# The query and key heads of a two-layer decoder trunk turned by VectorE in 32x32 blocks, where TensorE turned them before

## The reference

```python
h = rms_norm(x, g);  z = h @ w_in          # u, v, c_q, c_kv, k_rope, two gates
A = gelu(z_u) * (w_s @ layer_norm(gelu(z_v)) + b)
q = (rms_norm(c_q) @ w_uq).reshape(B, S, 16, 96)
kv = (rms_norm(c_kv) @ w_ukv).reshape(B, S, 16, 128)
k = concatenate([kv[..., :64], broadcast(k_rope)]);  v = kv[..., 64:]
q = rope(rms_norm(q));  k = rope(rms_norm(k))
p = softmax(causal(q @ k.T / sqrt(96)));  B = p @ v
x = x + (sig(g_A) * (A @ P_A) + sig(g_B) * (B @ P_B)) @ w_out
x = x + channel_mixer(rms_norm(x))
```

## Time and profile before

| | |
|---|---|
| time, median of 3 runs | 1435.28 us (1435.23 to 1435.92) |
| the profiled execution | 1435.76 us, span 1434.0 us |
| PE busy | 1424.2 us (99%) |
| DVE busy | 1143.0 us (80%) |
| ACT busy | 961.3 us (67%) |
| bytes moved | 415 MB |
| attention stretch of layer 0, first scores to pa 1 0 | 120.75 to about 190 us |
| the same in layer 1 | 427.7 us later |

### The profile page before, as it was taken

The page is one execution under the profiler, slowest core; times in us unless marked ns, Lnnn a source line. Parts: engine busy times, 40 slices in busy tenths (PEclk is TensorE's granted clock), DMA queues, the critical chain, the costliest instruction groups (busy, mean ns, idle before and its releaser), DMA issues.

```text
span 1434.0 us, 19208 instructions
## 1 busy us (share of the span) xinstructions
PE 1424.2 (99%) x6747; PEld 1178.5 (82%) x6747; DVE 1143.0 (80%) x1160; ACT 961.3 (67%) x1003; POOL 45.2 (3%) x54
## 2 busy tenths in 40 slices
PE   9999999999999999999999999999999999999998
PEld 7888778888888888778888888888888888888886
DVE  6987756665546977756989899898898988989987
ACT  6676754544435676754677787777777777777775
POOL 2000003000000000000200000000000000000200
PEclk9999999999999999999999999999999999999999
DMA  9473348955465473447899999999999999999994
GB/s 338 158 239 118 118 153 302 337 179 172 164 209 193 147 236 117 132 162 262 297 386 415 387 359 410 384 380 409 360 398 372 385 414 382 381 380 412 372 396 164
DMA packets 163267, 415.13 MB, mean 290 GB/s; under 512 B 15420, under 2 KB 43960, under 8 KB 163176
## 3 DMA queue, kind: packets, MB, share of 16 engines
q1 hardware_dynamic: 157128, 393.42, 74.3%
q0 software_dynamic: 5008, 16.97, 3.6%
q10 hardware_dynamic: 1040, 3.68, 0.6%
HBM read 398.20 MB, written 15.81 MB: 289 GB/s over the span
## 4 chain that ended last, share of the span: by engine, by line
PE 95%; ACT 2%; DVE 2%; issue 0%; POOL 0%; DVEq 0%; ACTq 0%; POOLq 0%
PE ps L551 88%; PE ps L1095 1%; PE ps L825 1%; PE ps L968 1%; PE ps L947 1%; PE ps L955 1%; PE ps L869 1%; ACT w_hi L506 1%; ACT qk_t L1238 1%; PE ps L934 0%; PE ps L903 0%; PE ps L946 0%; ACT prob L1363 0%; ACT sq L1363 0%; ACT act_hi L1238 0%
## 5 line engine op out<-in xcount | busy, mean ns | idle before, releaser
L511 DVE TENSOR_TENSOR w_lo<-raw,w_hi 128x2048 fp32r<-128x2048 f32 (+3 forms) x240 | 500.9, 2105 | 138.7 <-ACT w_hi L506 136.3
L506 ACT ACTIVATE w_hi<-raw 128x2048 fp32r<-128x2048 f32 (+3 forms) x240 | 421.8, 1769 | 185.2 <-PE ps L551 170.9
L551 PE MATMUL ps<-w_hi,act_hi 128*128 128x512 f32 (+1 forms) x1264 | 333.3, 392 | 0.7 <-ACT act_hi L1238 0.6
L551 PE MATMUL ps<-w_hi,act_lo 128*128 128x512 f32 (+1 forms) x1264 | 331.2, 388 | 0.0
L551 PE MATMUL ps<-w_lo,act_hi 128*128 128x512 f32 (+1 forms) x1264 | 327.4, 387 | 0.0
L551 PEld LDWEIGHTS ps<-w_lo,act_hi 128*128 128x128 f32 x1264 | 235.6, 188 | 48.2
L551 PEld LDWEIGHTS ps<-w_hi,act_lo 128*128 128x128 f32 x1264 | 234.9, 188 | 47.5
L551 PEld LDWEIGHTS ps<-w_hi,act_hi 128*128 128x128 f32 x1264 | 232.3, 188 | 47.2 <-ACT act_hi L1238 1.4
L511 DVE TENSOR_TENSOR w_lo<-raw_more,w_hi 128x2048 fp32r<-128x2048 f32 (+1 forms) x96 | 201.8, 2110 | 30.1 <-ACT w_hi L506 30.0
L506 ACT ACTIVATE w_hi<-raw_more 128x2048 fp32r<-128x2048 f32 (+1 forms) x96 | 170.0, 1776 | 55.2 <-PE ps L551 54.3
L511 DVE TENSOR_TENSOR w_lo<-raw_low,w_hi 128x2048 fp32r<-128x2048 f32 (+1 forms) x64 | 137.6, 2156 | 11.5 <-ACT w_hi L506 11.0
(11 more groups left out here) (284 smaller groups left out, 1231.4 us busy)
## 6 DMA issues: line engine op xcount, KB each, us to landing
raw<-in_moe_w_gu SPq DMA_DIRECT2D x128, 512.0 KB, 9.0
raw_more<-in_moe_w_down SPq DMA_DIRECT2D x80, 512.0 KB, 7.0
raw<-in_w_in SPq DMA_DIRECT2D x72, 512.0 KB, 4.6
raw_low<-in_moe_w_gu SPq DMA_DIRECT2D x64, 512.0 KB, 10.3
raw_more<-in_moe_w_gu SPq DMA_DIRECT2D x64, 512.0 KB, 10.5
raw<-in_moe_w_gu SPq DMA_DIRECT2D x64, 384.0 KB, 7.3
raw<-in_moe_w_down SPq DMA_DIRECT2D x48, 512.0 KB, 6.7
raw<-in_dense_w_gu SPq DMA_DIRECT2D x44, 512.0 KB, 5.0
```

Of the source, the lines that this page charges most:

```text
L506: nc.scalar.activation(w_hi[:, self.split_slot(j), 0:n], self.raw(j)[:, 0:n], ACT.Copy).then_inc(self.hi, 1)
L511: nc.vector.tensor_tensor(w_lo[:, c, 0:n], self.raw(j)[:, 0:n], w_hi[:, c, 0:n].bitcast(F32), ALU.subtract).then_inc(self.lo, 1)
L551: return nc.tensor.matmul(dst, a, b, start=start and n == 0, stop=stop and n == 2)
```

## The change

`qb` and `kb` get the layout [partition, token tile, group of 32 columns, head, 32], so that a head's three groups of 32 columns lie apart. In place of `qk_turns`:

- When the queries are ready, POOL issues 12 DMAs that move 32-partition pieces of `qb` to `q_blocks` (in SBUF, 128 KB each); then 12 for the keys of the first eight heads to `k_lent`, and 12 for the others to `k_last` (64 KB each). They put group g of a block of 32 tokens on the partitions 32g to 32g+31.
- DVE transposes 32x32 blocks in place (`blocks`): `q_blocks` in two halves of eight heads, `k_lent`, `k_last`, each 96 x 2048.
- ACT copies the turned queries with the gain to `q_first` and `q_second` (four heads each), and the other eight (`last_q`) to `q_last`. PE reads keys straight from `k_lent` and `k_last`.
- `k_lent` lies on the fourth raw slot, so that the chunks from u 0 0 to ga 1 4 have three slots; the first chunk that takes the slot again waits for the scores of pair 3.
- `q_rope` stands behind uq 2 and ukv 0 (before: behind ga 0 0 and ga 0 4), the squares of the queries' second half directly behind uq 2's reading, the squares of the keys' first half before the reading of ukv 2; `k_scale` stands behind ukv 3 and, ahead of that step's split, behind ga 0 0 (before: behind u 0 0 and gb 1 4). The reading of a uq strip takes ACT three instructions, `k_scale` three on DVE.
- In the first expert the load of the next expert's rows moves three steps later and the slot weights get a tile of their own.

```diff
-        mul(l, "uq", 2, 0, [evac("uq", 2)])
+        mul(l, "uq", 2, 0, [evac("uq", 2), ("head_squares", l, "q", 1), ("q_rope", l, 0)])
+        mul(l, "ukv", 0, 0, [("q_rope", l, 1), evac("ukv", 0)])
         plan.append(("head_sums", l, "q", 1))
-        mul(l, "ukv", 0, 0, [evac("ukv", 0)])
         mul(l, "ukv", 1, 0, [evac("ukv", 1)])
-        plan.append(("head_sums", l, "k", 0))
-        mul(l, "ukv", 2, 0, [evac("ukv", 2)])
-        mul(l, "ukv", 3, 0, [evac("ukv", 3)])
-        plan.append(("head_sums", l, "k", 1))
-        mul(l, "ga", 0, 0, [("mix_tokens", l, 0)])
-        plan.append(("q_rope", l, 0))
+        mul(l, "ukv", 2, 0, [("head_sums", l, "k", 0), evac("ukv", 2)])
+        mul(l, "ukv", 3, 0, [evac("ukv", 3), ("head_sums", l, "k", 1), ("k_scale", l, 0)])
+        mul(l, "ga", 0, 0, [("mix_tokens", l, 0), ("k_scale", l, 1)])
         mul(l, "ga", 0, 4, [("mix_tokens", l, 1), evac("ga", 0)])
-        plan.append(("q_rope", l, 1))
-        mul(l, "u", 0)
-        plan.append(("k_scale", l, 0))
-        mul(l, "u", 0, 4, [("u_arg", l, 0), ("split", l, len(chunks)), ("u_gelu", l, 0)], split=False)
-        mul(l, "u", 1, 0, [("branch", l, 0), *slot(1, exps=False)], inside=[(4, turn(0))], split=False)
-        mul(l, "u", 1, 4, [("u_arg", l, 1), *slot(2)], split=False,
-            inside=[(2, ("a_turns", l, 0)), (2, ("softmax", l, 0)), (5, turn(1)), (5, split())])
+        plan.append(("blocks", l, "q", 0))
+        mul(l, "u", 0, 0, [("blocks", l, "q", 1)])
+        mul(l, "u", 0, 4, [("u_arg", l, 0), ("split", l, len(chunks)), ("u_gelu", l, 0), ("blocks", l, "k", 0)], split=False)
+        mul(l, "u", 1, 0, [("branch", l, 0), *slot(1, exps=False)], split=False)
+        mul(l, "u", 1, 4, [("u_arg", l, 1), ("last_q", l, "q", 1), ("blocks", l, "k", 1), *slot(2)], split=False,
+            inside=[(2, ("a_turns", l, 0)), (2, ("softmax", l, 0)), (5, split())])
...
+                def move_heads(to, src, heads, moved):
+                    for b in range(4):
+                        for g in range(DG):
+                            pool.dma_start(to[32 * g:32 * g + 32, b:TT * 4:4, :, :], src[32 * b:32 * b + 32, :, g, heads, :]
+                                           ).then_inc(moved, 16)
+
+                pool.wait_ge(q_ready, TT * (l + 1))
+                move_heads(q_blocks, qb, slice(0, H), q_moved)
+                pool.wait_ge(lo_done, lent_read[l] + 1)
+                pool.wait_ge(k_ready, 2 * l + 1)
+                move_heads(k_blocks[0], kb, slice(0, 8), k_moved[0])
+                pool.wait_ge(k_ready, 2 * l + 2)
+                pool.wait_ge(q_moved, 16 * 4 * DG * (l + 1))
+                move_heads(k_blocks[1], kb, slice(8, H), k_moved[1])
...
-                    wait_turn_read(pe, qk_turn[l, pair])
-                    wait_turn_read(pe, qk_turn[l, pair] + 1)
+                    if pair % 4 == 0:
+                        pe.wait_ge(q_scaled, 2 * l + pair // 4 + 1)
+                        pe.wait_ge(k_turned, 2 * l + pair // 4 + 1)
...
+                elif kind == "blocks":
+                    half = step[3]
+                    if step[2] == "q":
+                        dve.wait_ge(q_moved, 16 * 4 * DG * (l + 1))
+                        part, done = q_blocks[0:DQ, :, 8 * half:8 * half + 8, :].rearrange("p b h i -> p b (h i)"), q_turned
+                    else:
+                        dve.wait_ge(k_moved[half], 16 * 4 * DG * (l + 1))
+                        part, done = k_blocks[half][0:DQ].rearrange("p b h i -> p (b h i)"), k_turned
+                    nc.vector.transpose(part, part).then_inc(done, 1)
```

More of the change, by code:

```diff
@@ L74, in decoder_trunk @@
     HR = DR // 2
+    DG = DQ // 32
     E = moe_w_gu.shape[1]
@@ L482, in split_slot, with wait_slot @@
                 return (self.n0 + j) % SPLIT
-            def load(self, sp, e, j, pieces):
+            def wait_slot(self, sp, e, j):
                 r = len(self.slots)
@@ L704, in expert_loads @@
                 for d in range(len(EDOWN_K)):
-                    if not last and d == 2:
-                        if q == 0 and is_first(e):
-                            sp.wait_ge(pass_sems[0]["slot_read"], 1)
+                    if not last and d == (ROWS_AT if q or not is_first(e) else FIRST_ROWS_AT):
+                        if not q and is_first(e):
+                            sp.wait_ge(rows_written, 16 * 2 * TT)
                         rows_load(q, e + 1)
@@ L1325, in _ @@
                     turn_hi_parts(b0, hid_hi, 2 * step[2], 1.0)
-                elif kind == "head_sums":
+                elif kind == "head_squares" or kind == "head_sums" and step[2:] != ("q", 1):
                     hf = step[3]
@@ L1366, in _ @@
                     op.then_inc(exp_done, 1)
-                elif kind == "qk_turns":
-                    pair, b = step[2], b0
-                    if pair:
-                        act.wait_ge(scores_done, PAIRS * l + pair)
-                    for hh in range(2):
-                        act.wait_ge(turn_done, b + hh + 1)
-                        if not l and not pair and not hh:
-                            act.wait_ge(qk_gain_ready, 1)
-                        copy(qk_t[0:DQ, hh, 0:S], ps[0:DQ, 4 + (b + hh) % 2, 0:S], qk_gain[0:DQ, l:l + 1])
-                        copy(qk_t[0:DQ, hh, S:2 * S], ps[0:DQ, 4 + (b + hh) % 2, S:2 * S]).then_inc(turn_free[(b + hh) % 2], 1)
+                elif kind == "last_q" or kind == "blocks" and step[2:] != ("q", 1):
+                    if step[2] == "q":
+                        half = step[3]
+                        act.wait_ge(q_turned, 2 * l + half + 1)
+                        if not l and not half:
+                            act.wait_ge(qk_gain_ready, 1)
+                        if half:
+                            for i in range(2):
+                                act.wait_ge(k_moved[i], 16 * 4 * DG * (l + 1))
+                        scale = qk_gain[0:DQ, l:l + 1]
+                        turned_blocks = q_blocks[0:DQ, :, 8 * half:8 * half + 8, :].rearrange("p b h i -> p h b i")
+                        for to, a in ((q_last, 0),) if half else ((q_first, 0), (q_second, 4)):
+                            n = to.shape[1]
+                            op = copy(to[0:DQ].rearrange("p h (b i) -> p h b i", i=32), turned_blocks[:, a:a + n], scale)
+                        op.then_inc(q_scaled, 1)
                 elif kind in ("split", "split_hi"):
@@ L1504, in slot_weights @@
                 def slot_weights(e):
-                    if q or not is_first(e):
-                        act.wait_ge(z["xw_landed"], 16 * gathers(q, e))
-                    else:
+                    if not q and is_first(e):
                         act.wait_ge(z["first_weights"], 16)
+                        copy(slot_w[:], xw_first[:, 0:1]).then_inc(z["slot_read"], 1)
+                        return
+                    act.wait_ge(z["xw_landed"], 16 * gathers(q, e))
                     copy(slot_w[:], xw[:, e:e + 1] if isinstance(e, int) else xw[:, bass.ds(e, 1)]).then_inc(z["slot_read"], 1)
@@ L1525, in body @@
                         split(e, c + LEAD, last)
-                        if c == SLOT_READ:
+                        if c == SLOT_READ and (q or not first):
                             slot_weights(e)
@@ L1533, in body @@
                             turn_part(e, EGS - 1)
+                        if first and not q and d == FIRST_SLOT_READ:
+                            slot_weights(e)
                         if not last and d in (6, 8):
```

170 lines of the change are left out of this document (109 added, 61 removed).

## The result

| | before | after |
|---|---|---|
| median | 1435.6 us (4 runs, 1435.23 to 1436.32) | 1444.24 us (4 runs, 1444.16 to 1445.21) |
| profiled span | 1434.0 us | 1442.4 us |
| granted clock, mean | 1.0 | 0.995 |

The account below looks back on a forecast made before the run. PE, busy 1424.2 of 1434.0 us, was taken as the bound. Per layer 1.5 + 5.0 + 1.4 - 0.3 + 0.5 - 7.1 = +1.0, two layers +2.0, clock +2.0: 1439.3 us, range 1430.5 to 1443.0.

Parts of the forecast that it names:

- What goes: PE's sets of eight transposes: 0.89 us saved a set, eight sets a layer, 7.1 us each, 14.2 us in all.
- Step 1: PE's wait at ga 0 0, in the banks of ukv 2, which ACT reads behind the key squares: +1.5 us a layer.
- Step 2: PE's wait before the first scores, from the DVE, ACT, DVE chain ending in the k_lent transpose: +5.0 us a layer.
- Step 3: PE's wait for pair 1's probabilities, with DVE transposing k_last ahead of the maximum: +1.4 us, old 0.3 wait included.
- Step 4: Shared banks: PE's second transposition of the probabilities waits longer for DVE's bt_lo, +0.5 us; later slots costed at no wait.
- Hidden: Moves of queries and keys, three slots instead of four, and first expert's loads: thought hidden, nothing costed.
- The clock: PE restarting at half clock after the 5 us stop loses about 2 us, taken in one of two layers: +2.0.
- The rival of both layers: PE restarts at the lower clock after the long wait in both layers: 1441.3 us; chance 0.14.
- that the clock holds: Rival: PE's waits stay but its clock does not fall behind them: 1437.3 us; chance 0.25.
- Cheap transposes: Rival: DVE transposes cost under 1.8 us (or chain shorter), pause under 3 us, clock holds: 1430.7 us; chance 0.20.
- Moves late: Rival: queries' moves land after DVE wants them, up to 5 us more a layer: 1447 us; chance 0.08.

Follow-up runs that it names:

- e3: Changed kernel with ACT reading ukv 2 from PSUM before it squares the keys; 1443.85 us, ratio 1.0045 to the kernel before.
- e7: Changed kernel with POOL holding the queries' moves until the low part of the split of ga 0 4 is done; 1450.71 us, ratio 1.0095.
- e4: Changed kernel, hand-over reordered: ACT splits u 1 4 before copying queries, DVE turns k_lent earlier, low part of gb 1 0 later; 1432.6 us, ratio 0.997.
- e8: Changed kernel with only DVE's turn of k_lent moved ahead of the addition for u 0's argument; 1439.19 us, ratio 1.0016.
- e2: Changed kernel with DVE's transpose of k_last moved from ahead of pair 1's maximum to behind pair 3's; 1441.9 us, ratio 1.0033.
- e1: Changed kernel with 40 unused transposes on PE ahead of the first scores of each layer; 1439.86 us, ratio 1.0025.
- e6: e4 with e2's edit, and q's second and k's head sums and two splits' low parts placed later; 1428.08 us, ratio 0.9934.
- e9: e8 with the edit of e2 (last keys turned late); 1435.79 us, ratio 0.9993 to the kernel before.
- e5: e4 with the edits of e2 and e3; 1428.83 us, ratio 0.9939 to the kernel before.

## Why the prediction was right and where it failed

**What goes:** right. From 159.55 to 193.47 four sets less give back 3.5 us (7.65 - 4.19), 0.87 a set against 0.89.

**Step 1:** the place and the releaser were right, the size nearly. Forecast +1.5, measured a wait of 1.70 and a shift of 2.05 at ga 0 0. The second square of the keys starts at 89.27 where 88.85 was worked out. e3 confirms the cause: with the reading ahead of the squares, ACT's `vv` releases nothing any more. But e3 also shows that this step and step 2 don't simply add: of the 0.8 us won here, 0.4 and 0.7 were left at the first scores.

**Step 2:** the chain was right link by link, its sum 1.3 us short: first scores at 127.66, forecast 126.3. 0.96 of that is there at its start (109.96 for 109.0): 0.55 from ga 0 0, and 0.4 because ACT comes to the split of u 1 0 late, behind the chunk that landed late (e7, without that delay, starts at 109.63). Of the other 0.4, the copies are 0.2: their steps were 1.07 and 1.03 us and not 0.93 each. The transposes were priced right: 2.28 to 2.30 us in the records, with steps of 2.2, as taken. The wait itself is 5.57 and 5.16 us against 5.0. e4 and e8 show that this chain was the largest single cost, and that it came from the order of two queues, not from the turns: e4 does all the same turns.

**Step 3:** right, 1.30 and 1.27 for 1.4; e2 removes it. **Step 4:** 0.44 in place of 0.17, so +0.3 a layer where 0.5 was taken, and from pa 0 0 on there is no wait, as costed.

**Hidden:** failed in part, though small. The queries' moves were in time (DVE turns at 112.17 right behind a split), but I asked only when they land and not what they do to others. The loads beside them land in 7.8 us (median) instead of 4.6, and one weighs on step 2, as e7 shows. The Trainium skill (SBUF — State Buffer, the section SBUF: two separate sides) warned of another thing, POOL kept from its descriptors by VectorE's copies in a two-port mode. The trace shows no sign of it, with the queries' 12 issues at 0.54 us each while DVE is busy 6.07 of 6.45 us; but DVE's work there is `tensor_tensor`, sums and a few operations on 32 columns, and no such copy, so it is hardly a test of the warning. The same section of the Trainium skill names the ports that the DMA engines share as the other place of contention. The longer landings would fit that, but no run here tells it from other causes in the transfers.

**The clock:** this is the step that failed. "I take it to happen in one of the two layers: +2.0." It happened in both, and cost 1.9 and 2.9 us, 4.8 in all; e1, which keeps PE busy in the same waits, has the clock at full speed and a span 4.0 us shorter. Of the miss of 4.4 us between the spans (1442.4 for 1438.0) the clock is 2.8. The rest is 1.6 (8.4 - 4.8 against 2.0): 0.6 of it are longer waits (17.7 - 0.9 = 16.8 for 16.2), and 1.0 is what the account above leaves over, whose cause is open. The rival of both layers, at 0.14 and 1441.3, had the mechanism. The one long stop in the trace before, its start, had matmuls at half speed behind it, and there was no row against it; the chance should have gone by that. (The evidence was the length of the transposes alone: the granted clock of that trace reads 1.00 from its first microsecond on.) The Trainium skill (TensorE: Matmul & The Clock Gate, What's actually happening) says that an idle PE drops to half the clock; for waits of 5 us the traces agree, in all eight of them (the changed kernel, e2, e3 and e7, two layers each). For waits below 3 us they don't settle it: the clock fell behind some and not behind others, as the last section shows.

**The rivals:** that the clock holds is refuted by the windows. Cheap transposes is refuted, 2.28 us being above its 1.8; its clock, taken to hold in a pause under 3 us, would not have been safe either, since in e6 it fell behind 2.44 us. Moves late is refuted for the queries themselves, which landed in time. The prediction held against it that the longest of the like rows was well below 19 us; the 12.9 us of the earlier trace rows is their median, and their longest took 21.4 us, so this argument was a misreading.

## What to carry to other kernels

Work taken from the engine that is the bound is worth only what its waits leave of it. Before moving it, write down both queues that feed the bound engine and ask of each entry between the last input and the hand-over whether it serves the next thing that engine does; here the order of a few entries was worth 13 us (e4), about as much as the 14 us of work that went. Give a stop of several us on TensorE its second price, the clock, in each place where it comes, and look also at what a new stream of transfers does to the loads beside it. A wait that is removed may show up again at the next one on the same path, in part or whole (e3, e6, e8): sum all waits before and after, not the one.

## What the runs showed of the hardware

- VectorE turned 96 x 2048 float32 in 32x32 blocks in 2.28 to 2.30 us, the time of its subtraction of 128 x 2048 (2.29), against 1.24 for one of 128 x 1024.
- SBUF to SBUF moves of 32 partitions (128 KB) landed in 6.7 us in the median. The four 512 KB weight loads issued beside them took 5.1 to 9.3 us to land, and 3.6 to 4.5 when the moves were held back (e7).
- The clock is not told by the length of the last wait alone. e9's layer 1 had waits of 0.70 and 2.91 us and kept the full clock; e8's layer 1, with 0.69 and 2.93 at the same places, fell to half. Rows of e9 and then of e8, layer 1:

```profile
557.00:558.00 1.00, 0.23 (x2) 1.00 0.79 248
558.00:559.00 1.00, 1.00 (x10) 1.00 1.03 395
```

```profile
558.00:559.00 1.00, 0.33 (x2) 0.64 0.94 272
559.00:560.00 1.00, 1.00 (x6) 0.50 1.04 401
```

Nor is it the kernel alone: the ten executions of e9 have mean granted clocks from 0.996 to 1.000, and their spans follow, 1432.3 to 1433.0 us at 1.000 and 1436.3 at 0.996; those of e8 lie between 0.995 and 0.999. A stop of 2.16 us (e5, layer 0) kept the full clock, and one of 2.18 (e9, layer 0) did not. What decides it no run here shows, but e9's time varied by 4 us from execution to execution with it.
